# Products of constants on TensorE while it waits, at the head of a two-layer decoder trunk and at three places of its first mixer

## The reference, cut to what matters

```
for l in range(DEPTH):                       # DEPTH = 2, x is (1, 256, 1024)
    x = x + 0.5 * swiglu(rms_norm(x, norm_w[l, 0]), ffn_w_gate[l, 0], ffn_w_up[l, 0], ffn_w_down[l, 0])
    h = rms_norm(x, norm_w[l, 1])
    if l % 2 == 0: x = x + mixer_mla_gdn(h, ...)      # the first mixer
    else:          x = x + mixer_spatial_gating(h, ...)
    x = x + 0.5 * swiglu(rms_norm(x, norm_w[l, 2]), ...)

# inside mixer_mla_gdn
q = apply_rope(rms_norm(q, qk_norm_q), cos, sin)     # 8 heads of 96
y_mla = causal_block_attention(q, k, v)              # softmax(q k^T) v in blocks of 128 queries
gk = l2_norm(gk)                                     # likewise gq; beta, g from two more projections
o = gated_delta_rule(gq, gk, gv, beta, g)            # chunks of 64: a triangular system, then 4 steps
y = concatenate([y_mla, rms_norm(o, out_norm) * silu(z)]) @ w_out
```

## Time and profile before

| | |
|---|---|
| runs of the kernel before | 1105.33, 1108.63, 1108.97 us (median 1108.63) |
| profiled execution, its own time | 1108.93 us |
| its span | 1107.1 us |
| TensorE busy with products | 1081.3 us, 98% of the span |
| VectorE, ScalarE, GpSimd busy | 647.3, 503.8, 47.1 us |
| mean granted TensorE clock | 0.994 |

### The profile page before, as it was taken

How to read it: one execution, slowest core, us unless ns; L and a number is a source line. 1 busy time by engine, 2 the same in 40 slices (tenths; PEclk the granted TensorE clock), 3 DMA queues, 4 the chain that set the end, 5 groups by cost and what they waited for, 6 DMA issues and landing times.

```text
span 1107.1 us, 18807 instructions
## 1 busy us (share of the span) xinstructions
PE 1081.3 (98%) x8329; PEld 987.0 (89%) x8329; DVE 647.3 (58%) x791; ACT 503.8 (46%) x597; POOL 47.1 (4%) x34
## 2 busy tenths in 40 slices
PE   7999999998889999999999999999999999999998
PEld 7999988987789799999889999888788889999986
DVE  5755544688665775555447555544764557555542
ACT  5644433683633354444335444434654536444430
POOL 1000000112051000000000000000100000000000
PEclk9999999999899999999999999999999999999999
DMA  9855555253002356555546565555445474665531
GB/s 311 265 181 187 189 190 178 87 190 114 1 15 68 126 184 189 188 190 191 190 152 194 188 190 191 190 185 176 153 159 218 155 228 154 192 189 190 191 114 38
DMA packets 127194, 184.91 MB, mean 167 GB/s; under 512 B 4205, under 2 KB 101722, under 8 KB 126986
## 3 DMA queue, kind: packets, MB, share of 16 engines
q1 hardware_dynamic: 126368, 181.88, 50.6%
q0 software_dynamic: 448, 1.71, 0.5%
q10 hardware_dynamic: 298, 0.12, 0.1%
HBM read 182.66 MB, written 1.05 MB: 166 GB/s over the span
## 4 chain that ended last, share of the span: by engine, by line
PE 88%; DVE 7%; ACT 2%; issue 2%; DMA 1%; POOLq 0%; SPq 0%; POOL 0%; DVEq 0%; ACTq 0%
PE B L1274 19%; PE B L1275 19%; PE B L1276 19%; PE B L1315 7%; PE B L1319 7%; PE B L1316 7%; PE B L1688 3%; DVE wlo L840 2%; DVE arena L1007 1%; PE B L1384 1%; PE B L1385 1%; PE B L1386 1%; DMA raw<-in_ffn_w_up 1%; PE B L1348 1%; PE B L1811 1%
## 5 line engine op out<-in xcount | busy, mean ns | idle before, releaser
L840 DVE TENSOR_TENSOR wlo<-raw,whi 128x2048 fp32r<-128x2048 f32 (+1 forms) x169 | 387.7, 2301 | 227.5 <-ACT whi L443 227.3
L443 ACT ACTIVATE whi<-raw 128x2048 fp32r<-128x2048 f32 (+1 forms) x171 | 324.2, 1908 | 385.2 <-PE B L1276 243.0
L1274 PE MATMUL B<-xTh,whi 128*128 128x256 f32 x1408 | 397.4, 282 | 0.3 <-DVE wlo L840 0.2
L1275 PE MATMUL B<-xTl,whi 128*128 128x256 f32 x1408 | 396.4, 282 | 0.0
L1276 PE MATMUL B<-xTh,wlo 128*128 128x256 f32 x1408 | 396.4, 282 | 0.0
L1274 PEld LDWEIGHTS B<-xTh,whi 128*128 128x128 f32 x1408 | 266.1, 189 | 1.2 <-DVE wlo L840 0.7
L1275 PEld LDWEIGHTS B<-xTl,whi 128*128 128x128 f32 x1408 | 266.3, 189 | 0.0
L1276 PEld LDWEIGHTS B<-xTh,wlo 128*128 128x128 f32 x1408 | 266.2, 189 | 0.0
L1315 PE MATMUL B<-whi,hTh 128*128 128x512 f32 x352 | 139.5, 396 | 0.0
L1316 PE MATMUL B<-wlo,hTh 128*128 128x512 f32 x352 | 139.0, 395 | 0.0
L1319 PE MATMUL B<-whi,hTl 128*128 128x512 f32 x352 | 110.6, 395 | 0.0
(11 more groups left out here) (241 smaller groups left out, 999.6 us busy)
## 6 DMA issues: line engine op xcount, KB each, us to landing
raw<-in_ffn_w_up SPq DMA_DIRECT2D x44, 1024.0 KB, 5.4
raw<-in_ffn_w_down SPq DMA_DIRECT2D x44, 1024.0 KB, 4.8
raw<-in_ffn_w_gate SPq DMA_DIRECT2D x43, 1024.0 KB, 5.5
raw<-in_sg_w_in SPq DMA_DIRECT2D x16, 1024.0 KB, 5.4
raw<-in_ab_w_in SPq DMA_DIRECT2D x8, 1024.0 KB, 5.1
raw<-in_sg_w_out SPq DMA_DIRECT2D x8, 1024.0 KB, 5.3
raw<-in_ab_w_out SPq DMA_DIRECT2D x4, 1024.0 KB, 4.8
raw<-in_ab_w_in SPq DMA_DIRECT2D x2, 832.0 KB, 4.4
```

Source lines behind the costliest of these rows:

```text
L443: A(whi[:, j % SLOTS, 0:kt * width], raw[:, j % SLOTS, 0:kt * width], ACT.Copy).then_inc(S("hi_ready"), 1)
L840: TT(wlo[:, j % SLOTS, 0:n], raw[:, j % SLOTS, 0:n], whi[:, j % SLOTS, 0:n].bitcast(f32), ALU.subtract).then_inc(S("lo_ready"), 1)
L1274: mm(out_ap, lh, rh, start=first, stop=False)
L1275: mm(out_ap, lh, rl, start=False, stop=False)
```

## The change

One new helper, `keep_awake(bank, left, right, count)`, issues `count` products of 128 x 128 by 128 x 256 of type f32 into a bank that nobody reads at that time. It is called at five points of TensorE's program:

- ahead of everything: 5 products from `arena[:, 0:384]` into bank 5, behind a wait for a memset that VectorE now does first
- between the transposes of the second and of the third quarter of x: 1 product
- between `to_tokens(5)` and `qk_transposes(4)`: 6 products of `ident` by `C` into bank 7
- in round 0, ahead of the wait for `y_mla`: 4 products into bank 7
- in round 0, ahead of the wait for `yT_lo`: 4 products into bank 4

The semaphore `begc_ready`, for which nobody waited, goes; in its place VectorE's own wait for that instruction (`link`) stands.

```diff
--- before.py
+++ after.py
@@ -951,6 +951,7 @@
                     for q in range(4):
                         x_update(s, q, factor)
 
+            nc.vector.memset(arena[:, 0:384], 1.0).then_inc(S("warm_ready"), 1)
             link(nc.vector.memset(rs_a, 0.0))
             dve.wait_ge(S("pos_loaded"), 16)
             nc.vector.tensor_copy(pos_rows[:, 1, :], pos_rows[:, 0, :].bitcast(i32)).then_inc(S("pos_float"), 1)
@@ -1123,7 +1124,7 @@
                     TS(Dec, Dec, 0.0, None, ALU.max).then_inc(S("dec_diff"), 1)
                 if h == 2:
                     dve.wait_ge(S("decay_exps"), 2)
-                    TT(begc, beta, egc, ALU.mult).then_inc(S("begc_ready"), 1)
+                    link(TT(begc, beta, egc, ALU.mult))
                     dve.wait_ge(S("dec_exp"), 1)
                     TT(m3(DecB), m3(Dec), bc(beta.rearrange("p t h -> p (t h)").unsqueeze(2), [P, M, 64]), ALU.mult
                        ).then_inc(S("decb_ready"), 1)
@@ -1448,10 +1449,19 @@
                 down(s, base + 22, 11, hidden=PAIRS_F * f)
 
 
+            def keep_awake(bank, left, right, count):
+
+                for _ in range(count):
+                    mm(B[bank][:, 0:256], left, right, start=True, stop=True)
+
+            pe.wait_ge(S("warm_ready"), 1)
+            keep_awake(5, arena[:, 0:128], arena[:, 128:384], 5)
             pe.wait_ge(S("ident_loaded"), 16)
             pe.wait_ge(S("norm_loaded"), 16)
             transpose(B[7][:, 0:48], norm_rows[:], ident[0:48, 0:48]).then_inc(S("norm_sums"), 1)
             for t, n in ((0, 0), (1, 0), (0, 1), (1, 1)):
+                if (t, n) == (0, 1):
+                    keep_awake(5, arena[:, 0:128], arena[:, 128:384], 1)
                 pe.wait_ge(S(f"x_loaded{t}{n}"), 16)
                 for k in range(4 * n, 4 * n + 4):
                     last = transpose(B[X_BANK[k // 2]][:, 256 * (k % 2) + P * t:256 * (k % 2) + P * t + P],
@@ -1559,6 +1569,7 @@
                 qk_transposes(i)
             gemm(Z_UNIT + 1, (0, 1), 4, KD, XS)
             to_tokens(5)
+            keep_awake(7, ident, C[:, 0:256], 6)
             for i in range(4, 8):
                 qk_transposes(i)
 
@@ -1699,6 +1710,7 @@
                         pe.wait_ge(S("d_ready"), t + 1)
                     problems(t, 4 + t, LT, D).then_inc(S("m1_sums"), 1)
                 if n == 0:
+                    keep_awake(7, ident, C[:, 0:256], 4)
                     pe.wait_ge(S("y_mla"), 2)
                     pe.wait_ge(S("dT_out"), 4)
                     y_transposes(0, 4)
@@ -1712,6 +1724,7 @@
                         problems(t, 6 + t, DT, M1).then_inc(S("y_sums"), 1)
                     problems(t, t, M1, DT).then_inc(S("yt_sums"), 1)
                 if n == 0:
+                    keep_awake(4, ident, C[:, 0:256], 4)
                     pe.wait_ge(S("yT_lo"), 4)
                     gram(qT, (2, 3))
                 if n == 1:
```

## The result

The changed kernel takes 1109.52 us (median of 14 runs, 1107.53 to 1110.96), the kernel before 1107.78 us (14 runs, 1105.33 to 1109.09). The ratio is 1.0017 with a 95% interval of 1.0010 to 1.0024: 1.7 to 1.9 us slower. The forecast was 1106.7 us, faster. The profiled execution took 1110.96 us with a span of 1109.2, which is 2.1 us more than the span of before.

What follows compares the result with a forecast made beforehand. TensorE, busy 98% of the span, was taken as the bound, paying twice for falls to 1.2 GHz. 1108.93 + 0.0 + 0.0 - 0.2 - 1.7 + 0.0 = 1107.0, against the median 1106.7 us; range 1103.9 to 1110.1.

Steps and rivals of the forecast that it cites:

- Does it reach the end?: Behind 324 us: TensorE and VectorE in turn, then SwiGLU without a hole, weights loaded ahead; all the gain passed on.
- The head: Products 1 to 5 and one more at the start: only idle time ahead of 18.43 us gained, 0.0 us.
- Place 2: Six products ahead of `qk_transposes(4)`: hidden by ScalarE, clock fall moved to 286 to 289 us rather than removed, -0.2 us.
- The ScalarE cover: ScalarE's `qkT_out(4)` comes at 279.15 only, transposes end at 279.05, so the six products ahead of them are hidden.
- Place 3: Four products ahead of `y_mla`: no clock fall at 318.5 us, 128 records in 3.8 rather than 5.45 us, -1.7 us.
- Place 4: Four products ahead of `yT_lo`: they fit the 2.1 us hole, where the clock did not fall; 0.0 us.
- Rival 3: First unit: TensorE, faster, idles half the time up to 14.3 us and the clock falls; 1110.0 us, chance 0.13.
- Rival 2: Products don't keep the clock up, or executions fall elsewhere; only 0.2 us won, 1108.4 us, chance 0.22.
- Rival 1: Clock holds through the scores despite 3.2 us idle, giving 1.9 us more: 1104.8 us, chance 0.21.
- the rule that I set against the change: Transposes don't count as clock activity, so those behind the added products leave TensorE as good as idle and the clock falls.

Runs made afterwards that it cites:

- head_only: Kernel before plus only the memset, its wait and the 5 + 1 products at the head, none in the mixer; 1108.47 us, ratio 1.0006.
- after_l2: Changed kernel with the two 1 MB weight loads held back until v_sums = 4; 1106.62 us, ratio 0.9994 to the kernel before.
- mixer_l2: Changed kernel without its head part, with the two 1 MB weight loads held back until v_sums = 4; 1106.13 us, ratio 0.9991 to the kernel before.
- before_l2: Kernel before with the two 1 MB weight loads held back until v_sums = 4; 1107.22 us, ratio 0.9997.
- late_loads: Changed kernel with the two 1 MB weight loads held back until w_sums = 2 (some 355 us); 1107.70 us, ratio 1.0003 to the kernel before.
- filled_l2: mixer_l2 plus 6 keep_awake products behind head_scores(1); 1104.87 us, ratio 0.9971 to the kernel before.
- pad_l2: Kernel before plus 20 two-column products ahead of qk_transposes(4), two 1 MB loads held back until v_sums = 4; 1109.43 us, ratio 1.0024.
- p3_l2: before_l2 plus only the 4 products ahead of the wait for y_mla; 1107.94 us, ratio 0.9996 to the kernel before.
- mixer_only: Changed kernel without its head part (no memset, no products around the first transposes); 1110.05 us, ratio 1.0026 to the kernel before.
- after: The changed kernel itself, with all five calls, against the kernel before; 1109.52 us, ratio 1.0017.

## Why the prediction was wrong

**The step that failed** is "Does it reach the end?", in which I wrote of the part behind 324 us "then SwiGLU blocks with TensorE busy without a hole. The weights are loaded ahead, with `raw` waits only at the head. I pass all of it on." I looked for what the weights would wait for, not for what their loads do to others. TensorE was in the least sheltered part of the kernel, four rounds of 64 x 64 products in 0.030 us a record, and two 1 MB loads ran over it. The kernel before got through by the place at which its blocks of instructions fell; the 20 added products, each two records with a weight load apiece (80 instructions), moved them. The term is +2.8 us in the profile, +2.9 in the medians (1109.52 against 1106.62). I had no rival for it: all three were about the clock. The Trainium skill ("Runtime: NRT & Kernel Launch", section Instruction fetch mechanics) says that the sequencer refills its instructions in blocks of 16 KB by a DMA queue of its own, and that crossing a block's edge is mostly hidden. The trace agrees on the blocks (4 of q8 with 0.07 MB in the view above) but not, here, on the hiding, and the sign of the result hung on it. With the loads out of the way the change gives -0.6 us (1106.62 against 1107.22) and not -1.9; the other 1.3 us, no more than such medians can tell for sure, fit the falls of the clock, below.

**The head, 0.0:** right as far as it can be measured. head_only is +0.7 us with an interval that holds zero, and after_l2 is 0.5 us over mixer_l2. `blocks(1)` did start early in the profile, by 0.4 us, but because its weights landed early, and in before_l2 and late_loads they did as well (`lo(1)` at 14.91 and 15.07 us instead of 16.08), so this is no doing of the products.

**Place 2, -0.2 and the fall moved:** right in mechanism and size for this profile. The idle stretch of 3.2 us was there, 0.50 stood behind it at 289.6 to 292.8, and the profile gives -0.2. filled_l2 shows the reason: fill that stretch too, and the clock stays. The ScalarE cover held with the first transposes at 279.39.

**Place 3, -1.7:** -1.55 in this profile, but not what it is worth over many executions. By itself it measured 1107.94 us; the whole mixer part, with the loads out of the way, -1.1 us (1106.13 against 1107.22, with intervals of 1.0 and 1.2 us to either side). I took one execution's falls for fixed. They are not: the changed kernel has one at 269 us, where the kernel before does the same work at 1.00, and it costs 1.5 us. It stands in the profiles of late_loads and pad_l2 too, of which pad_l2 has no product at the head, and not in that of after_l2, which has them; so nothing here ties it to the change. The mean clock of the profiled execution, which has two falls, is 0.997, and eight of the fourteen have that value; so two falls may well be the rule here, but only profiles tell where they lie.

**Place 4, 0.0:** right for the profile I had, wrong as an account of the call. p3_l2 shows the fall that it guards against.

**Rival 3** (a fall in the first unit) did not come in the changed kernel: TensorE was busy for 2.85 of 4.15 us there, idle for a third and not for half, and 1.00 stayed to 269 us. It did come in mixer_only, which has no products at the head, so it is a risk of that stretch and not of the change. **Rival 2** fails in its first half on the view of windows: 1.00 from 316 to 323 us. Its other half, that executions fall elsewhere, is part of what happened. **Rival 1** did not happen in this kernel and does in filled_l2.

**Two readings.** Rows 1 show one slice of the clock under 9, not two. And the window from 264.46 to 269.73 is weaker evidence than I made it: the same 20 transposes are followed by 0.50 at 269 us in three other profiles (after, late_loads, pad_l2), so the one trace did not refute the rule that I set against the change. What speaks against its use here is that the clock held behind the transposes of lines 1564 and 1689 once products stood ahead of them.

**What stays open:** why a block that falls due within a load is served 2 us late in one case and 3.3 in another; and whether it waits for one of the DMA engines or for something else. No experiment tells these apart. Nor is it known why one idle stretch of 2 us brings a fall and another does not, nor why the fall at 269 comes in some executions.

## What to carry to other kernels

Where TensorE runs many small products, look for weight loads that are under way at that time and for blocks of the instruction queue; a change that adds instructions anywhere ahead moves those blocks, and can cost or give 2 to 3 us by that alone. Hold back loads that nobody needs yet, before trying anything fine in such a stretch, and compare changes only after that. Filling idle stretches to keep the clock pays best when all long ones of the chain are filled (-3.1 us here, with the two loads held back as well); filling one can move the fall to the next and win nothing (p3_l2). Look at more than one execution before you price a fall.

## What the runs showed of the hardware that I had not expected

- One 16 KB block lasts TensorE 3.8 us in these rounds: some 127 records of products at 0.030 us with as many weight loads. Of a block's lateness it absorbed 1.0 to 1.4 us, so little is fetched ahead. Where it stopped, it went on 2.4 to 2.7 us after the block had started.
- A stall of 2.00 us was followed by 3.2 us at 0.50, so late instructions can cost the clock as well (mixer_only).
- A product of 128 x 128 weights with 2 columns is not small: 20 of them, 40 records, took 4.53 us.
